# A decoder layer on one core: the block series of the delta rule in the other order, its diagonal inverse turned on VectorE and applied last, and log and exp of each root from one set of tables

## The reference, cut to what matters

```python
kk = jnp.einsum('bhncd,bhnsd->bhncs', k, k)
A = jnp.where(strict, beta[..., :, None] * kk * decay, 0.0)
sol = lax.linalg.triangular_solve(eye + A, rhs, left_side=True, lower=True)
u, w = sol[..., :Dv], sol[..., Dv:]
# per chunk, with the state S
u_new = u_c - w_c @ S
o = (q_c * exp(G_c)) @ S + qk_c @ u_new
S = S * exp(G_last) + (k_c * exp(G_last - G_c)).T @ u_new
```

## Time and profile before

| | |
|---|---|
| three executions | 2581.53, 2587.45, 2582.7 us; median 2582.7 |
| profiled execution | 2588.41 us, its span 2586.7 us |
| granted TensorE clock, mean | 0.992 |
| busy: TensorE matmuls | 2546.2 us (98%) |
| busy: DVE, ACT, POOL | 1662.3, 1321.6, 510.2 us |
| chain that ended last | TensorE 92%, DVE 2%, DMA 2%, POOL, ACT and issue 1% each |

### The profile page before, as it was taken

The page is one execution under the profiler, slowest core; times in us unless marked ns, Lnnn a source line. Parts: engine busy times, 40 slices in busy tenths (PEclk is TensorE's granted clock), DMA queues, the critical chain, the costliest instruction groups (busy, mean ns, idle before and its releaser), DMA issues.

```text
span 2586.7 us, 50475 instructions
## 1 busy us (share of the span) xinstructions
PE 2546.2 (98%) x20848; PEld 2525.4 (98%) x20848; DVE 1662.3 (64%) x2862; ACT 1321.6 (51%) x2013; POOL 510.2 (20%) x912
## 2 busy tenths in 40 slices
PE   8999999999999999999999999999999999999997
PEld 7999999999999999999999999999999999999997
DVE  5767777686777765433365566566776656776665
ACT  6545646464655644333244344445665545665664
POOL 1527163452716340000000000200110000110100
PEclk8999999999999999999999999999999999999999
DMA  7656565555656556677755566757986768986563
GB/s 210 180 146 192 144 174 154 160 167 155 183 147 176 152 164 196 177 211 213 205 167 180 179 200 200 242 178 250 320 277 216 220 189 254 311 283 189 167 204 116
DMA packets 445718, 507.38 MB, mean 196 GB/s; under 512 B 21329, under 2 KB 423914, under 8 KB 443066
## 3 DMA queue, kind: packets, MB, share of 16 engines
q1 hardware_dynamic: 417072, 415.43, 53.1%
q0 software_dynamic: 27840, 88.53, 11.3%
q10 hardware_dynamic: 578, 0.19, 0.0%
HBM read 478.16 MB, written 26.49 MB: 195 GB/s over the span
## 4 chain that ended last, share of the span: by engine, by line
PE 92%; DVE 2%; DMA 2%; POOL 1%; ACT 1%; issue 1%; DVEq 0%; POOLq 0%; ACTq 0%
PE bank L700 91%; DMA raw<-in_w_ffn_down 1%; DVE wlo L1364 1%; POOL sol L555 1%; POOL prod L552 1%; ACT whi L1033 1%; DMA raw<-in_w_ple_gate 0%; PE bank L791 0%; PE bank L780 0%; DMA blk<-blk_scratch 0%; ACT sqr L1272 0%; DMA DT<-sol_scratch 0%; DVE xlo L1404 0%; ACT xhi L1332 0%; PE bank L724 0%
## 5 line engine op out<-in xcount | busy, mean ns | idle before, releaser
L700 PE MATMUL bank<-xhi,whi 128*128 128x264 f32 x5520 | 1591.9, 288 | 7.2 <-DVE wlo L1364 4.2
L700 PE MATMUL bank<-xlo,whi 128*128 128x264 f32 x5520 | 1569.0, 284 | 0.0
L700 PE MATMUL bank<-xhi,wlo 128*128 128x264 f32 x5520 | 1566.5, 284 | 0.0
L1364 DVE TENSOR_TENSOR wlo<-raw,whi 128x1024 fp32r<-128x1024 f32 x828 | 1013.5, 1231 | 727.6 <-ACT whi L1033 726.9
L1033 ACT ACTIVATE whi<-raw 128x1024 fp32r<-128x1024 f32 x828 | 872.5, 1057 | 810.9 <-PE bank L700 743.6
L700 PEld LDWEIGHTS bank<-xhi,whi 128*128 128x128 f32 x5520 | 1041.8, 189 | 10.3 <-issue 6.6
L700 PEld LDWEIGHTS bank<-xlo,whi 128*128 128x128 f32 x5520 | 1042.5, 189 | 2.0 <-issue 1.9
L700 PEld LDWEIGHTS bank<-xhi,wlo 128*128 128x128 f32 x5520 | 1039.3, 188 | 0.0
L700 PE MATMUL bank<-ahi,whi 128*128 128x264 f32 x704 | 200.1, 284 | 2.5 <-DVE wlo L1364 2.5
L700 PE MATMUL bank<-ahi,wlo 128*128 128x264 f32 x704 | 200.1, 284 | 0.0
L700 PE MATMUL bank<-alo,whi 128*128 128x264 f32 x704 | 199.7, 284 | 0.0
(11 more groups left out here) (306 smaller groups left out, 1827.4 us busy)
## 6 DMA issues: line engine op xcount, KB each, us to landing
raw<-in_w_in SPq DMA_DIRECT2D x356, 512.0 KB, 4.1
raw<-in_w_ffn_gate SPq DMA_DIRECT2D x88, 512.0 KB, 5.2
raw<-in_w_ffn_up SPq DMA_DIRECT2D x88, 512.0 KB, 4.7
raw<-in_w_ffn_down SPq DMA_DIRECT2D x96, 384.0 KB, 3.5
raw<-in_w_gdn_out SPq DMA_DIRECT2D x64, 512.0 KB, 3.5
chunkS<-in_state_gdn POOLq DMA_DIRECT2D x16, 1024.0 KB, 7.4
raw<-in_w_sconv_out SPq DMA_DIRECT2D x32, 512.0 KB, 3.5
raw<-in_w_o SPq DMA_DIRECT2D x32, 512.0 KB, 4.4
```

The source lines that it names most:

```text
L700: return pe.matmul(out, lhsT, rhs, start=start, stop=stop)
L1364: dve.tensor_tensor(wlo[:, at_ % SPLIT, :, :], raw[:, at_ % RAW, :, :], f32(whi[:, at_ % SPLIT, :, :]), ALU.subtract).then_inc(lo_ready, 1)
```

## The change

The series is done on V itself and D is applied last: `u = D*(I + P')(I + P'^2)*v` with `P'` from `D*N` in place of `N*D`. `nturn` (8 transposes a group), `ncopy` (2 copies), `t0`, `t0c`, `t1`, `t1c` go. DVE turns `DT` block by block of 32x32 into `Nn` (`dturn`, piece 26, one instruction on [128, 1024]), and `pt` waits for it (`dn`). `ud0` and `ud1` (4 matmuls each) with ACT's copies `u0c` and `u1c` come behind `u0` and `u1`. By that `s1` moves from piece 31 to 0, `ks` from 0 to 1, `o1` from 5 to 6, `osum` from 7 to 8, and with them `s1c`, `o0c`, `r`, `osq`, `s2`, `oroot`, `o`. `qroot` and `oroot` load the table set `natural_log_exp_and_others` ahead of their waits.

```diff
-        PE_STEP = {"cur": {5: ("kk",), 10: ("nturn",), 11: ("qsum",), 15: ("qk",), 18: ("tails",), 19: ("vturn",),
-                           27: ("pt",), 28: ("pt0",), 29: ("pe0",), 30: ("pf0",), 31: ("s1",)},
-                   "prev": {0: ("ks",), 1: ("t1",), 2: ("pt1",), 3: ("pe1",), 4: ("pf1",), 5: ("o1",), 7: ("osum", "sct")},
+        PE_STEP = {"cur": {5: ("kk",), 11: ("qsum",), 15: ("qk",), 18: ("tails",), 19: ("vturn",),
+                           27: ("pt",), 28: ("pt0",), 29: ("pe0",), 30: ("pf0",), 31: ("ud0",)},
+                   "prev": {0: ("s1",), 1: ("ks",), 2: ("pt1",), 3: ("pe1",), 4: ("pf1",), 5: ("ud1",), 6: ("o1",), 7: ("sct",), 8: ("osum",)},
-        ACT_STEP = {"cur": {1: ("exps",), 5: ("kcopy",), 10: ("qsq",), 11: ("ncopy",), 12: ("qroot",),
-                            19: ("stage",), 20: ("vcopy",), 27: ("t0c",), 29: ("f0c",), 31: ("s1c",)},
-                    "prev": {0: ("o0c",), 1: ("t1c",), 3: ("f1c",), 6: ("osq",), 7: ("oroot",), 8: ("sct",)},
+        ACT_STEP = {"cur": {1: ("exps",), 5: ("kcopy",), 10: ("qsq",), 12: ("qroot",),
+                            19: ("stage",), 20: ("vcopy",), 29: ("f0c",)},
+                    "prev": {0: ("u0c",), 1: ("s1c",), 2: ("o0c",), 3: ("f1c",), 6: ("u1c",), 7: ("osq",), 8: ("sct", "oroot")},
-        DVE_STEP = {"cur": {5: ("lt",), 13: ("qn",), 16: ("qkt",), 27: ("mask",), 28: ("e0",),
+        DVE_STEP = {"cur": {5: ("lt",), 13: ("qn",), 16: ("qkt",), 26: ("dturn",), 27: ("mask",), 28: ("e0",),
-                    "prev": {0: ("r",), 2: ("e1",), 4: ("u1",), 6: ("s2",), 9: ("o",)},
+                    "prev": {1: ("r",), 2: ("e1",), 4: ("u1",), 7: ("s2",), 10: ("o",)},
...
                     pe.wait_ge(g["dt_in"], gr * 64 + 64)
+                    pe.wait_ge(g["dn"], gr + 1)
                     for c in range(NCH):
-                        for i, s in enumerate(heads):
-                            m = mm(B[4 + c][:, s], Nn[:, c, s], DT[:, 4 * c + i, :])
+                        for s in heads:
+                            m = mm(B[4 + c][:, s], Nn[:, c, s], Tt[:, c, s])
                     m.then_inc(g["pt"], 1)
-                    for i, s in enumerate(heads):
-                        m = mm(B[6][:, s], DT[:, i, :], vTok[:, 0, i, :])
-                    m.then_inc(g["t0"], 1)
...
+                elif slot == "ud0":
+                    pe.wait_ge(g["u0"], gr + 1)
+                    for i, s in enumerate(heads):
+                        m = mm(B[4][:, s], DT[:, i, :], Tt[:, 0, s])
+                    m.then_inc(g["ud0"], 1)
                 elif slot == "s1":
-                    pe.wait_ge(g["u0"], gr + 1)
+                    pe.wait_ge(g["u0c"], gr + 1)
                     for s in heads:
-                        mm(B[5][:, s], Nn[:, 0, s], Tt[:, 0, s])
-                        m = mm(B[6][:, s], Tt[:, 0, s], QK[:, 0, s])
+                        mm(B[5][:, s], Nn[:, 0, s], cs[:, 0, s])
+                        m = mm(B[6][:, s], cs[:, 0, s], QK[:, 0, s])
...
                 elif slot == "qroot":
+                    act.preload_act_table_set("natural_log_exp_and_others")
                     act.wait_ge(g["qsum"], gr + 1)
...
+                elif slot == "u0c":
+                    act.wait_ge(g["ud0"], gr + 1)
+                    act.activation(cs[:, 0, :], bank[4][:, :], ACT.Copy).then_inc(g["u0c"], 1)
...
                 elif slot == "oroot":
+                    act.preload_act_table_set("natural_log_exp_and_others")
                     act.wait_ge(g["osum"], gr + 1)
...
-                            dve.wait_ge(g["o1"], gr)
+                            dve.wait_ge(g["ud1"], gr)
...
+                elif slot == "dturn":
+                    dve.wait_ge(g["dt_in"], gr * 64 + 64)
+                    dve.transpose(Nn[:, :, :].rearrange("p c t -> p (c t)"), DT[:, :, :].rearrange("p m t -> p (m t)")).then_inc(g["dn"], 1)
...
-                    dve.tensor_tensor(Tt[:, 0, :], bank[7][:, :], cs[:, 0, :], ALU.add).then_inc(g["e0"], 1)
+                    dve.tensor_tensor(Tt[:, 0, :], bank[7][:, :], vTok[:, 0, :, :].rearrange("p i v -> p (i v)"), ALU.add).then_inc(g["e0"], 1)
```

More of the change, by code:

```diff
@@ L263, in trunk @@
             "kk", "ksq", "klog", "klen", "qsq", "qsum", "qlog", "qroot", "qn", "qk", "qkt",
[L264 to L267, removed]
+            "rows", "gb", "expo", "dt", "kcopied", "lt",
+            "blk_stored", "blk_in", "solved", "sol_stored", "dt_in", "dn", "vturned", "vcopied", "pt", "masked",
+            "pt0", "e0", "pe0", "f0c", "pf0", "u0", "ud0", "u0c", "s1", "s1c", "ks", "r",
+            "pt1", "e1", "pe1", "f1c", "pf1", "u1", "ud1", "u1c", "o1", "s2", "stored",
             "osq", "osum", "olog", "oroot", "o")}
@@ L741, in gdn @@
                 heads = [slice(i * CH, i * CH + CH) for i in range(4)]
+                vflat = vTok[:, :, :, :].rearrange("p c i v -> p c (i v)")
                 def apply(out, vec_, c):
@@ L772, in gdn @@
                     m.then_inc(g["qk"], 1)
[L773 to L781, removed]
                 elif slot == "tails":
-                    pe.wait_ge(g["ncopied"], gr + 1)
                     pe.wait_ge(silu_done, 4 * gr + 4)
@@ L788, in gdn @@
                     pe.wait_ge(g["qkt"], gr + 1)
+                    pe.wait_ge(g["kcopied"], gr + 1)
+                    if gr > 0:
+                        pe.wait_ge(sct_staged, gr)
                     for c in range(NCH):
@@ L796, in gdn @@
                     pe.wait_ge(g["dt_in"], gr * 64 + 64)
+                    pe.wait_ge(g["dn"], gr + 1)
                     for c in range(NCH):
-                        for i, s in enumerate(heads):
-                            m = mm(B[4 + c][:, s], Nn[:, c, s], DT[:, 4 * c + i, :])
+                        for s in heads:
+                            m = mm(B[4 + c][:, s], Nn[:, c, s], Tt[:, c, s])
                     m.then_inc(g["pt"], 1)
-                    for i, s in enumerate(heads):
-                        m = mm(B[6][:, s], DT[:, i, :], vTok[:, 0, i, :])
-                    m.then_inc(g["t0"], 1)
                 elif slot == "pt0":
                     pe.wait_ge(g["masked"], gr + 1)
-                    pe.wait_ge(g["t0c"], gr + 1)
-                    apply(B[7], cs, 0).then_inc(g["pt0"], 1)
+                    apply(B[7], vflat, 0).then_inc(g["pt0"], 1)
                 elif slot == "pe0":
@@ L824, in gdn @@
                     m.then_inc(g["ks"], 1)
-                elif slot == "t1":
+                elif slot == "pt1":
                     pe.wait_ge(g["r"], gr + 1)
[L827 to L832, removed]
+                    apply(B[4], vflat, 1).then_inc(g["pt1"], 1)
                 elif slot == "pe1":
@@ L838, in gdn @@
                     apply(B[4], cs, 1).then_inc(g["pf1"], 1)
-                elif slot == "o1":
+                elif slot == "ud1":
                     pe.wait_ge(g["u1"], gr + 1)
                     for i, s in enumerate(heads):
+                        m = mm(B[7][:, s], DT[:, 4 + i, :], Tt[:, 1, s])
+                    m.then_inc(g["ud1"], 1)
+                elif slot == "o1":
+                    pe.wait_ge(g["u1c"], gr + 1)
+                    for i, s in enumerate(heads):
                         mm(B[7][:, s], S[:, i, :], EG[:, gr % 2, i, :], True, False)
-                        mm(B[7][:, s], Tt[:, 1, s], QK[:, 1, s], False, True)
-                        m = mm(B[4][:, s], Nn[:, 1, s], Tt[:, 1, s])
+                        mm(B[7][:, s], cs[:, 1, s], QK[:, 1, s], False, True)
+                        m = mm(B[4][:, s], Nn[:, 1, s], cs[:, 1, s])
                     m.then_inc(g["o1"], 1)
@@ L1102, in gdn @@
                     act.activation(kTok[:, :, :, :].rearrange("p a b c -> p (a b c)"), bank[6][:, :], ACT.Copy).then_inc(g["kcopied"], 1)
[L1103 to L1106, removed]
                 elif slot == "stage":
@@ L1121, in gdn @@
                     m.then_inc(g["vcopied"], 1)
[L1122 to L1127, removed]
+                elif slot == "f0c":
+                    act.wait_ge(g["pe0"], gr + 1)
+                    act.activation(cs[:, 0, :], bank[6][:, :], ACT.Copy).then_inc(g["f0c"], 1)
+                elif slot == "f1c":
+                    act.wait_ge(g["pe1"], gr + 1)
+                    act.activation(cs[:, 1, :], bank[5][:, :], ACT.Copy).then_inc(g["f1c"], 1)
+                elif slot == "u0c":
+                    act.wait_ge(g["ud0"], gr + 1)
+                    act.activation(cs[:, 0, :], bank[4][:, :], ACT.Copy).then_inc(g["u0c"], 1)
+                elif slot == "u1c":
+                    act.wait_ge(g["ud1"], gr + 1)
+                    act.activation(cs[:, 1, :], bank[7][:, :], ACT.Copy).then_inc(g["u1c"], 1)
                 elif slot == "s1c":
@@ L1502, in gdn @@
                     dve.wait_ge(g["pt1"], gr + 1)
-                    dve.tensor_tensor(Tt[:, 1, :], bank[4][:, :], cs[:, 1, :], ALU.add).then_inc(g["e1"], 1)
```

(1 more changed line is left out.)

## The result

The changed kernel takes 2588.69 us (median of 20 executions, 2585.54 to 2596.98) against 2583.52 us (20 executions, 2579.43 to 2587.45): ratio 1.0022, 95% interval 1.0016 to 1.0029, so 5.2 us slower. That lies inside the range given and just beyond the 0.2% that bounds "no change"; the forecast itself was +0.8 us, and "slower" had a chance of 0.20. The two profiled executions thus rank the kernels the wrong way round, and what matters has to be read group by group.

A forecast was written before the change was run, and what follows sets the result against it. The prediction took TensorE's queue to bound the kernel in groups 1 to 7. Group 0 +2.0, groups 1 to 6 -0.7 and group 7 -0.5 gave +0.8 us on the median 2582.7: 2583.5 us, range 2576.5 to 2591.

The forecast's parts named there:

- TensorE's work: TensorE's queue: eight transposes (`nturn`) removed, 0.87 us gained a group, at most 7.0 us in all.
- The turn: DVE's transposition of `DT`: taken as 1.2 us, after a full pass over 128x1024 float32 of 1.23 us.
- the reciprocal's pace: Rival, chance 0.04: DVE's transposition takes 7.0 us, `pt` is 4.7 us late in seven groups: +40 us, 2623.
- hidden, with 1.1 us to spare: Groups 1 to 7: DVE's transposition ends at 254.4, before `pt` wants it at 255.55, covered by pieces 26 and 27.
- The other moved steps: Steps shifted to other pieces, such as `ks`, `u1c`, `sct`, `osum`: no stall, thinly, with 0.6 us of room at piece 15.
- (A): TensorE at a group's end waits for DVE's `e0`, since `t0` no longer stands before piece 28: 0.4 us.
- (B): TensorE at `s1` waits for ACT's `u0c`, delayed behind DVE's exponents: 0.35 us, absent after group 7.
- The root as the bound: Rival, chance 0.17: TensorE waits at piece 15 for DVE's split, 0.7 us or more in seven groups: 2589.
- Group 0 and the base: Group 0, where `pt` already waits for `DT`: +2.0 us; the summed difference was put on the median, 2582.7.
- the slow clock: Group 0: after a longer stall the half clock may stand from the first matmul: +0.3 us, between -0.3 and +1.3.
- The sum: All groups: group 0 +2.0, groups 1 to 6 -0.7, group 7 -0.5, together +0.8 us.

The follow-up runs named there:

- the second execution: Both kernels run once more with nothing changed, one execution each: 2582.43 us for the kernel before, 2587.31 us for the changed kernel.

## Why the prediction was right or wrong

**TensorE's work: right.** 0.87 us a group, confirmed from both sides: 1.75 us with the transposes doubled, groups of 113.51 us with all stalls gone.

**The turn: right in size, wrong in cover.** It took 1.25 us for 1.2. The estimate of 2.5 us from the table in the Trainium skill (VectorE: DVE Perf Modes, "The three transpose paths") was twice that, and the reciprocal's pace is out. The step that failed is "hidden, with 1.1 us to spare". It took the landing from the kernel before and a median transfer, and set it against a DVE that would be free at 253.2. In groups 1 to 7 of the changed kernel DVE waited for `DT` four times, up to 2.65 us, and in group 2 of the second execution 3.5 us. The 1.1 us itself was too small: it left out that `ud1` now stands behind `kk`, so that `pt` stays 73.6 us behind `kk`. With the root back the turn ended at 71.5 us, 2.1 us ahead of `pt`; the late landing used up more than that.

**The other moved steps: the step that failed.** I wrote that `sct` ahead of the root "lets POOL start its solve about 2 us earlier: no gain". In the kernel before with the root alone moved it was 4 us. But in five of the six groups that were late in the two executions of the changed kernel the solve began between 0.6 us earlier and 0.3 us later than in the kernel before. There the last store of the diagonal blocks, issued 8.1 us after `kk` as before, landed at 12.8 to 13.8 us where it had landed at 11.1 to 11.9, and the stores behind it went out later; the cause of that is open. And I costed the later `o` on ACT, DVE and TensorE only. What it does to POOL, 3 us on the solve, was nowhere, though POOL's rows of 0.24 and 1.1 us for like work stood in the trace. Both come down on `pt`: it was 2.2 us late in sum over groups 1 to 6 of one execution and 2.5 in the other.

**Stalls (A) and (B): right.** 0.43 us in eight groups against 0.40, 0.38 in groups 1 to 6 against 0.35, none after group 7. In group 0 both were there too, (B) with 0.72.

**The root as the bound: priced about right, not come.** The preload took the second load away, 8 loads to 6 a group, and TensorE met piece 15 without a wait. With the loads left the kernel before paid 0.55 us in each of six groups, where I had 0.7 or more in seven.

**Group 0 and the base: wrong footing.** I put +2.0 us there and carried it to the median, though the execution shown was the one with the longest wait of several: 116.24 us from `kk` to `kk` against 111.47, 113.56 and 110.61 in other executions of kernels whose group 0 is the same but for the root's loads. The four small transfers are not all of it: in the execution shown the granted clock was also 0.50 for some 3 us at the first `kk`, and `DT`'s last issue came 1.5 us later after `kk` than in the execution of 2582.43 us. Against that one the two changed ones lose 1.5 and 1.8 us in group 0 (112.1 and 112.4 us, and 0.9 for `ud1`, which moved behind the next `kk`); the +2.0 was near, for other reasons than the slow clock.

**The sum.** For the second execution of both: group 0 +1.8, groups 1 to 6 +2.7, group 7 -0.4 by its steps: +4.1 of the 4.9 us between the two executions; the rest lies outside the groups. The forecast had +2.0, -0.7, -0.5. Of the 3.4 us that groups 1 to 6 are above it, 2.5 are `pt` behind a late `DT`. So the term that failed is this wait, put at nothing in groups 1 to 7. That 2588.69 us still lies in the range is luck: its upper end was drawn for the root, whose stall did not come. I haven't tested the port itself (a solve with DVE held still), nor `o` apart from the root ahead of it, only when both run; that the shared resource is what the two engines fight for is read from rows that stand side by side.

## What to carry to other kernels

When a step moves, look at every engine that works beside it at its new place, also at one off the critical path: here an elementwise step on VectorE, a piece later, slowed GpSimd, and through two rounds of transfers the bound. Whether it counts depends on when that engine's chain can begin, so the chain has to be followed from its first transfer. Work put behind a landing takes over all of the landing's spread, so its room has to be read from the latest landing and not from the median. And work that leaves the bound engine's queue may have been the cover of a chain elsewhere: 0.9 us moved from before `pe0` opened a stall of 0.43, which a later mask of the half not yet needed closed again.

## What had not been expected of the hardware

A GpSimd instruction of 30 elements took 0.24 us alone and 1.1 us beside a VectorE one with two SBUF inputs; a solve of 62 small instructions ran 34.6 or 37.5 us by where the outputs' root and the VectorE step behind it stood. And group 0 of one and the same kernel took 111.47 or 116.24 us, by its small transfers and the granted clock: TensorE's wait was 1.88 us in one execution and 3.77 in the other, where the granted clock then was 0.50 for some 3 us.
